# Two hand-overs between mixer and MLP, done by token block in a two-block decoder kernel

## What is computed

```python
# first block
y = mixer(rmsnorm(x, norm_mix_pre), ...)              # ends in  y @ w_out
x = x + rmsnorm(y, norm_mix_post)                     # hand-over 1
h = rmsnorm(x, norm_ffn_pre)
u = dwconv3(h @ w_up, conv_w)                         # 1024 -> 2 x 2816, width-3 taps over tokens
gate, val = jnp.split(u, 2, axis=-1)
y = (jax.nn.silu(gate) * val) @ w_down
x = x + rmsnorm(y, norm_ffn_post)                     # hand-over 2
# second block
proj = rmsnorm(x, norm_mix_g) @ w_in                  # its mixer goes on from here
```

## Time and profile before

| | us |
|---|---|
| median of 3 runs | 684.61 (683.48 to 685.54) |
| the profiled execution | 682.7 |
| its span, first to last instruction | 680.7 |
| TensorE busy | 637.0 (94%) |
| VectorE busy | 379.1 (56%) |
| ScalarE busy | 277.7 (41%) |
| GpSimd busy | 56.1 (8%) |

### The profile page before, as it was taken

The page is one execution under the profiler, slowest core; times in us unless marked ns, Lnnn a source line. Parts: engine busy times, 40 slices in busy tenths (PEclk is TensorE's granted clock), DMA queues, the critical chain, the costliest instruction groups (busy, mean ns, idle before and its releaser), DMA issues.

```text
span 680.7 us, 11095 instructions
## 1 busy us (share of the span) xinstructions
PE 637.0 (94%) x4347; PEld 482.7 (71%) x4347; DVE 379.1 (56%) x666; ACT 277.7 (41%) x431; POOL 56.1 (8%) x81
## 2 busy tenths in 40 slices
PE   7999999999999999999999999999999987668895
PEld 4999997799999999996598788744444432315364
DVE  5696965768766666666769456352222221203195
ACT  6763373656555555545774831220111110000193
POOL 1000000400000000002074620000000000000010
PEclk9999999999999999999999999999999998898998
DMA  9943542747655555302933448899899999999931
GB/s 323 328 172 126 194 141 67 267 149 243 235 186 185 185 185 186 128 0 101 392 142 123 139 172 320 350 430 428 354 430 430 425 425 428 428 428 427 405 128 62
DMA packets 55208, 174.75 MB, mean 257 GB/s; under 512 B 4742, under 2 KB 29442, under 8 KB 48898
## 3 DMA queue, kind: packets, MB, share of 16 engines
q1 hardware_dynamic: 54496, 172.54, 66.2%
q10 hardware_dynamic: 674, 1.69, 0.7%
HBM read 173.17 MB, written 1.05 MB: 256 GB/s over the span
## 4 chain that ended last, share of the span: by engine, by line
PE 73%; DMA 14%; DVE 7%; ACT 2%; issue 2%; another core or an unknown queue 0%; POOL 0%; POOLq 0%; DVEq 0%; ACTq 0%
PE ps L1809 15%; PE ps L1811 15%; PE ps L1810 15%; DMA W<-in_w_moe_dram 7%; DMA spare<-in_w_moe_dram 6%; PE ps L2326 6%; PE ps L2310 3%; PE ps L2386 3%; PE ps L2332 2%; PE ps L2006 2%; PE ps L1781 1%; PE ps L2433 1%; PE ps L2154 1%; DVE arena L1466 1%; PE ps L2105 1%
## 5 line engine op out<-in xcount | busy, mean ns | idle before, releaser
L1809 PE MATMUL ps<-hT_high,w_up_parts 128*128 128x256 f32 x352 | 99.9, 284 | 0.0
L1811 PE MATMUL ps<-hT_high,w_up_parts 128*128 128x256 f32 x352 | 99.7, 283 | 0.0
L1810 PE MATMUL ps<-hT_low,w_up_parts 128*128 128x256 f32 x352 | 99.7, 283 | 0.0
L1809 PEld LDWEIGHTS ps<-hT_high,w_up_parts 128*128 128x128 f32 x352 | 67.6, 192 | 0.5
L1810 PEld LDWEIGHTS ps<-hT_low,w_up_parts 128*128 128x128 f32 x352 | 67.6, 192 | 0.4
L1811 PEld LDWEIGHTS ps<-hT_high,w_up_parts 128*128 128x128 f32 x352 | 67.6, 192 | 0.0
L1297 DVE TENSOR_TENSOR w_up_parts<-W,w_up_parts 128x1024 fp32r<-128x1024 f32 x44 | 53.2, 1235 | 24.3 <-ACT w_up_parts L826 24.3
L826 ACT CAST w_up_parts<-W 128x1024 fp32r<-128x1024 f32 x44 | 44.7, 1047 | 28.5 <-PE ps L1811 28.5
L2326 PE MATMUL ps<-W,junk 128*32 128x512 f32 x368 | 46.2, 630 | 7.5 <-DMA W<-in_w_moe_dram 7.5
L996 ACT ACTIVATE sg<-ps 128x256 f32<-128x256 f32 x9 | 3.5, 384 | 121.4 <-PE ps L2326 121.4
L1809 PE MATMUL ps<-h_high,dense_high 128*128 128x256 f32 x160 | 45.8, 286 | 0.0
(11 more groups left out here) (480 smaller groups left out, 1318.7 us busy)
## 6 DMA issues: line engine op xcount, KB each, us to landing
W<-in_w_moe_dram SPq DMA_DIRECT2D x22, 2048.0 KB, 21.1
arena<-in_w_moe_dram SPq DMA_DIRECT2D x14, 2048.0 KB, 30.0
W<-in_w_up_dram SPq DMA_DIRECT2D x22, 1024.0 KB, 8.8
W<-in_w_in_dram SPq DMA_DIRECT2D x8, 2048.0 KB, 10.9
W<-in_w_down_dram SPq DMA_DIRECT2D x11, 1024.0 KB, 5.1
spare<-in_w_moe_dram SPq DMA_DIRECT2D x5, 2048.0 KB, 20.7
hh<-in_w_moe_dram SPq DMA_DIRECT2D x4, 2048.0 KB, 32.7
W<-in_w_out_dram SPq DMA_DIRECT2D x2, 2048.0 KB, 9.3
```

Source lines behind the costliest of these rows:

```text
L1809: pe.matmul(o, lhs[0], rhs[0], start=first, stop=False, skip_group_check=True)
L1810: pe.matmul(o, lhs[0], rhs[1], start=False, stop=False, skip_group_check=True)
L1811: return pe.matmul(o, lhs[1], rhs[0], start=False, stop=last_k, skip_group_check=True)
```

## The change

On TensorE the w_out products are ordered so that block 0 is complete after 60 of its 96 matmuls; block 0 is turned inside block 1's products, and the dummies go. The first MLP pair is not made by `up` any more: `up_tokens` has the tokens of one block stationary and 512 (block 0) or 2 x 256 (block 1) weight columns moving, ScalarE copies the result u out of PSUM into `junk` (`copy_up`), and `turn_up` turns it into the banks in which pair 0's taps read it. For block 0 that stands ahead of `turn_h(1, 1)`; block 1's last turns stand behind the first chunk of pair 1. The last two pairs' down products go by block, with those of the pair before (`down_before`) mixed in. In the second hand-over block 1 is turned within block 0's product, and that product begins with one written-out half. Dummies there: 4 ahead of the turn and 6 behind it. Both roots of a hand-over take the second half's sum as their bias. On VectorE the turned halves of block 0 are written out and lowered at the end of block 0's part (r = 0). Not shown in the diff: the new semaphores `u_done`, `uc_ready`, `u_turned`; y1's high part moves to another place in the arena; GpSimd builds its selection constants behind the split of pair 9 instead of behind `mlp_done` (its three edge fills stay there); pair 0's split is no longer cut in two, and `conv_mlp(0)` on ScalarE doesn't split pair 1, which is done ahead of it.

```diff
...
@@ -723,17 +723,17 @@
     act.wait_ge(sig("yms_ready"), n + 1)
-    act.activation(stat[:, 42 + 4 * r + b:43 + 4 * r + b], stat[:, 40 + 4 * r + b:41 + 4 * r + b], ACT.Sqrt)\
-       .then_inc(sig("ystd_ready"), 1)
-    if b == 1 and r == 0:
-        round_h(0)
+    act.wait_ge(sig("ysq_ready"), 2 * n + 2)
+    act.activation(stat[:, 42 + 4 * r + b:43 + 4 * r + b], stat[:, 40 + 4 * r + b:41 + 4 * r + b], ACT.Sqrt,
+                   bias=stat[:, 61:62]).then_inc(sig("ystd_ready"), 1)
...
     act.wait_ge(sig("xms_ready"), n + 1)
-    act.activation(stat[:, c + 2:c + 3], stat[:, c:c + 1], ACT.Sqrt).then_inc(sig("std_ready"), 1)
+    act.wait_ge(sig("xhsq_ready"), 2 * n + 2)
+    act.activation(stat[:, c + 2:c + 3], stat[:, c:c + 1], ACT.Sqrt, bias=stat[:, 63:64]).then_inc(sig("std_ready"), 1)
@@ -825,12 +825,28 @@
-split_up(0, 0, 0, (0, 1))
+split_up(0, 0, 0)
...
     hand_over(0, b)
-act.dma_start(gbc[:], a["norm_ffn_post"][0:1, :].broadcast_to([P, D])).then_inc(sig("gbc_landed"), 16)
-for j in range(1, 4):
-    round_h(j)
+    if b == 1:
+        act.dma_start(gbc[:], a["norm_ffn_post"][0:1, :].broadcast_to([P, D])).then_inc(sig("gbc_landed"), 16)
+    else:
+        round_h(0)
+        round_h(1)
+def copy_up(n, b, c0, c1):
+    act.wait_ge(sig("u_done"), at("u_done", n))
+    act.copy(junk[:, 512 * b + c0 * P:512 * b + c1 * P], ps[:, 5 if b and not c0 else 4, c0 * P:c1 * P]).then_inc(sig("uc_ready"), 1)
+copy_up(1, 0, 0, 4)
+round_h(2)
+round_h(3)
+copy_up(2, 1, 0, 2)
+split_up(1, 1, 0, (0, 1))
+copy_up(3, 1, 2, 4)
+split_up(1, 1, 0, (2, 3))
+act.wait_ge(sig("u_turned"), at("u_turned", 1))
@@ -868,13 +882,19 @@
 act.wait_ge(sig("down_landed0"), (NPAIR // 2) * 16 + 16)
-for i in range(2):
+def last_down(i):
...
     act.copy(last_dn[0][i], DN[0][:, i]).then_inc(sig("down_high"), 1)
+last_down(0)
+for i in range(2):
...
         act.activation(c[:, i, :], ps[:, i, 256 * g:256 * g + 256], ACT.Copy, scale=w).then_inc(sig("centre_done"), 1)
+    if i == 0:
+        last_down(1)
@@ -1129,12 +1149,11 @@
                 dve.wait_ge(sig("ysq_ready"), 2 * n + 1)
+                dve.tensor_scalar(stat[:, 40 + 4 * r + b:41 + 4 * r + b], stat[:, 60:61], EPS, None,
+                                  ALU.add).then_inc(sig("yms_ready"), 1)
...
                               ALU.mult).then_inc(sig("yg_ready"), 1)
-        dve.wait_ge(sig("ysq_ready"), 2 * n + 2)
-        dve.scalar_tensor_tensor(stat[:, 40 + 4 * r + b:41 + 4 * r + b], stat[:, 60:61], EPS, stat[:, 61:62], ALU.add,
-                                 ALU.add).then_inc(sig("yms_ready"), 1)
-        if b == 1:
+        if b == 1 and r == 1:
@@ -1147,18 +1166,21 @@
         c = 4 * (r + 1) + b
-        dve.wait_ge(sig("xhsq_ready"), 2 * n + 2)
-        dve.scalar_tensor_tensor(stat[:, c:c + 1], stat[:, 62:63], EPS, stat[:, 63:64], ALU.add,
-                                 ALU.add).then_inc(sig("xms_ready"), 1)
-        if b == 1 and r == 0:
-            lower_h(0)
+        dve.wait_ge(sig("xhsq_ready"), 2 * n + 1)
+        dve.tensor_scalar(stat[:, c:c + 1], stat[:, 62:63], EPS, None, ALU.add).then_inc(sig("xms_ready"), 1)
...
                           ALU.mult).then_inc(sig("hn_ready"), 1)
-    turn_out(r + 1, gain, 2)
-    turn_out(r + 1, gain, 3)
+        if r == 0:
+            for j in (2 * b, 2 * b + 1):
+                turn_out(r + 1, gain, j)
+            for j in (2 * b, 2 * b + 1):
+                lower_h(j)
+    if r == 1:
+        turn_out(r + 1, gain, 2)
+        turn_out(r + 1, gain, 3)
@@ -1928,42 +1953,75 @@
 pe.wait_ge(sig("sgo_ready"), at("sgo_ready", 2))
-for half in range(2):
-    for b in range(TB):
-        for k in range(4):
-            pe.wait_ge(sig("dense_low"), 4 * (6 + half) + k // 2 + 1)
-            product(ps[:, 4 + 2 * b + half, :], [t[:, k, b * P:(b + 1) * P] for t in y1],
-                    [t[:, k, :] for t in panel_hl(6 + half)], k == 0, False)
-for b in range(TB):
-    pe.wait_ge(sig("y1_low"), b + 2)
-    for half in range(2):
-        for k in range(4, KD):
-            pe.wait_ge(sig("dense_low"), 4 * (6 + half) + k // 2 + 1)
-            last = product(ps[:, 4 + 2 * b + half, :], [t[:, k, b * P:(b + 1) * P] for t in y1],
-                           [t[:, k, :] for t in panel_hl(6 + half)], False, k == KD - 1)
-    last.then_inc(sig("y_done"), 1)
+def out_rows(b, half, ks):
+    for k in ks:
+        pe.wait_ge(sig("dense_low"), 4 * (6 + half) + k // 2 + 1)
+        last = product(ps[:, 4 + 2 * b + half, :], [t[:, k, b * P:(b + 1) * P] for t in y1],
+                       [t[:, k, :] for t in panel_hl(6 + half)], k == 0, k == KD - 1)
+    return last
+out_rows(0, 0, range(4))
+out_rows(1, 0, range(4))
+out_rows(0, 1, range(4))
+pe.wait_ge(sig("y1_low"), 2)
+out_rows(0, 0, range(4, KD))
+out_rows(0, 1, range(4, KD)).then_inc(sig("y_done"), 1)
+out_rows(1, 1, range(4))
+pe.wait_ge(sig("y1_low"), 3)
+out_rows(1, 0, range(4, KD))
 turn_h(1, 0)
-keep_busy(3, 8)
-for k in range(24):
-    pe.matmul(ps[:, 3, 0:P], y1[0][:, k % KD, 0:P], y1[0][:, k % KD, 0:P], start=True, stop=True, skip_group_check=True)
+out_rows(1, 1, range(4, KD)).then_inc(sig("y_done"), 1)
+u_tok = v3(junk[:], TB)
+def up_tokens(b, c0, c1):
+    pe.wait_ge(sig("up_low"), c1)
+    for k in range(KD):
+        if k % 4 == 0:
+            pe.wait_ge(sig("hT_low"), 2 * b + k // 4 + 1)
+        last = product(ps[:, 5 if b and not c0 else 4, c0 * P:c1 * P], [t[:, k, b * P:(b + 1) * P] for t in hT_hl],
+                       [t[:, c0:c1, k, :] for t in w_up_hl], k == 0, k == KD - 1)
+    return last
+def turn_up(b, c0, c1):
+    for c in range(c0, c1):
+        i, g = divmod(c, 2)
+        last = pe.transpose(ps[:, i, 256 * g + b * P:256 * g + (b + 1) * P], u_tok[:, b, c * P:(c + 1) * P], ident[:])
+    return last
+up_tokens(0, 0, 4).then_inc(sig("u_done"), 1)
 turn_h(1, 1)
-pe.wait_ge(sig("hT_ready"), 4 + 2)
-keep_busy(0, 8)
 pe.wait_ge(sig("x_ready"), 2)
-for n in range(4):
-    pe.matmul(ps[:, 4 + n, :], zb[:, 0:P], zb[:], start=True, stop=False, skip_group_check=True)
-def up(p, q):
-    if not (isinstance(p, int) and p == 0):
-        pe.wait_ge(sig("tap_done"), p * 8 - 7)
+for n in range(2):
+    pe.matmul(ps[:, 6 + n, :], zb[:, 0:P], zb[:], start=True, stop=False, skip_group_check=True)
+pe.wait_ge(sig("uc_ready"), at("uc_ready", 1))
+turn_up(0, 0, 4)
+for h in range(2):
+    last = up_tokens(1, 2 * h, 2 * h + 2)
+    last.then_inc(sig("u_done"), 1)
+    pe.sem_inc(sig("up_used"), 2)
+def last_turns():
+    pe.wait_ge(sig("uc_ready"), at("uc_ready", 2))
+    turn_up(1, 0, 2)
+    pe.wait_ge(sig("uc_ready"), at("uc_ready", 3))
+    turn_up(1, 2, 4).then_inc(sig("u_turned"), 1)
+    for n in range(2):
+        pe.matmul(ps[:, 4 + n, :], zb[:, 0:P], zb[:], start=True, stop=False, skip_group_check=True)
+def up(p, q, behind_first=None):
+    pe.wait_ge(sig("tap_done"), p * 8 - 7)
     for c in range(4):
+        if c == 1 and behind_first:
+            behind_first()
...
         for k in range(KD):
-            if isinstance(p, int) and p == 0 and c == 0 and k % 4 == 0:
-                pe.wait_ge(sig("hT_low"), 3 + k // 4)
@@ -1978,31 +2036,59 @@
 pe.sem_inc(sig("down_used"), 1)
-up(0, 0)
-with pe.Fori(0, NPAIR // 2) as i:
+up(1, 1, last_turns)
+down(0, 0)
+up(2, 0)
+down(1, 1)
+with pe.Fori(1, NPAIR // 2 - 1) as i:
...
     down(i * 2 + 1, 1)
-for b in range(TB):
-    for i in range(2):
-        pe.wait_ge(sig("uact_low"), NPAIR + i)
-        pe.wait_ge(sig("down_low"), 2 * (NPAIR - 1) + i + 1)
-        for half in range(2):
-            last = product(ps[:, 4 + 2 * b + half, :], [t[:, 0, i, b * P:(b + 1) * P] for t in uact_hl],
-                           [t[i][:, 512 * half:512 * half + 512] for t in last_dn], False, True)
-    last.then_inc(sig("y_done"), 1)
+up(NPAIR - 2, 1)
+down(NPAIR - 3, 0)
+up(NPAIR - 1, 0)
+def down_before(b, i, halves):
+    pe.wait_ge(sig("uact_low"), NPAIR - 1)
+    pe.wait_ge(sig("down_low"), 2 * (NPAIR - 2) + i + 1)
+    for half in halves:
+        product(ps[:, 4 + 2 * b + half, :], [t[:, 1, i, b * P:(b + 1) * P] for t in uact_hl],
+                [t[:, i, 512 * half:512 * half + 512] for t in w_dn_hl], False, True)
+def down_last(b, i):
+    pe.wait_ge(sig("uact_low"), NPAIR + i)
+    pe.wait_ge(sig("down_low"), 2 * (NPAIR - 1) + i + 1)
+    for half in range(2):
+        last = product(ps[:, 4 + 2 * b + half, :], [t[:, 0, i, b * P:(b + 1) * P] for t in uact_hl],
+                       [t[i][:, 512 * half:512 * half + 512] for t in last_dn], False, True)
+    return last
+down_before(0, 0, range(2))
+down_before(0, 1, range(2))
+down_last(0, 0)
+down_before(1, 0, range(2))
+down_before(1, 1, range(1))
+down_last(0, 1).then_inc(sig("y_done"), 1)
+down_before(1, 1, range(1, 2))
+down_last(1, 0)
+down_last(1, 1).then_inc(sig("y_done"), 1)
...
 pe.wait_ge(sig("a2_landed"), 16)
-keep_busy(0, 16)
-for b in range(TB):
-    turn_h(2, b)
-    pe.wait_ge(sig("hT_ready"), 4 * 2 + 2 * b + 2)
+keep_busy(0, 4)
+turn_h(2, 0)
+keep_busy(3, 6)
```

(5 more changed lines are left out.)

28 lines of the change are left out of this document (12 added, 16 removed).

## The result

| | before | changed |
|---|---|---|
| median of the runs | 684.74 us (683.48 to 685.54) | 674.01 us (673.63 to 674.45) |
| ratio to before, 95% interval | | 0.9841 [0.9826, 0.9856] |
| profiled execution (span) | 682.7 (680.7) | 674.45 (672.4) |

Faster by 10.7 us in the medians and by 8.3 us between the two profiled executions. The forecast was 677.0, its range 674.0 to 681.5: 3 us too high, and the time lies at the range's lower edge (as a share of before it is just past it: 0.9841 against 674.0 / 684.61 = 0.9845). The gain of 10.7 us is also more than the 9.5 that the prediction gave as its upper bound.

What follows compares the result with a forecast made beforehand. Experts were taken as bound by weights, the MLP by TensorE, with two hand-overs leaving TensorE without useful work. Gains 5.1 + 2.5 = 7.6 us off 682.7 give 675.1, plus 1.9 to the median: 677.0, range 674.0 to 681.5.

Steps and rivals of the forecast that it cites:

- the last step of the sum: From the expected profiled execution, 675.1 us, to the median: 1.9 us added as in the kernel before, giving 677.0.
- the upper bounds of both hand-overs: Most that the two hand-overs could gain: 6 us in the first and 3.5 in the second, up to 9.5.
- First hand-over: From w_out to the MLP: first down product at 147.8 instead of 152.98, gain 5.1 us, bounds 3 to 6.
- The wait in (g): First MLP pairs: first down product waits 1.3 us for pair 0's lowered activation, whose taps now follow pair 1's split.
- The roots: Chain inside both hand-overs: VectorE's sum ahead of each root goes, 0.2 us each, twice per block; 5.6 us becomes 5.2.
- Second hand-over: From the MLP to mixer 2: xm products begin at 334.35 instead of 336.86, gain 2.5 us, bounds 0.5 to 3.5.
- GpSimd's constants: Moved into the MLP, about 274.5: 2.2 us of delay against 5.2 us of slack, so free; x updates undisturbed.
- SyncE's late reload: Reload for pair 2 issued at 137.2 instead of 135.96, landing at 146: hidden, with 5 us or so to spare.
- One gain only: Rival: second hand-over's gain is lost in the mixer behind it, or half of the first is; 679.5 us, chance 0.22.
- nothing arrives: Rival: the weight stream takes back the lead, or fuller first hand-over queues lag 5 us; 684.6 us, chance 0.08.
- Slower, by the clock: Rival: with forty dummies gone, TensorE's clock falls in pairs 0 and 1, costing up to 17 us; 694 us, chance 0.05.

Runs made afterwards that it cites:

- after_again: The changed kernel, unchanged, timed and profiled once more: 674.36 us, ratio 0.9851.
- old_order: Changed kernel with 12 w_out products moved ahead, so y's block 0 is complete after 72 products, not 60: 678.74 us, ratio 0.9913.
- no_C: Changed kernel with GpSimd's selection constants built after the end of the MLP again, as before: 675.58 us, ratio 0.9867.
- early_taps: Changed kernel with VectorE's copy of pair 0's conv taps ahead of pair 1's split and block 1's turns inside chunk 0: 673.28 us, ratio 0.9845.
- no_A: Kernel before with all of the change but the first hand-over's part: 680.29 us, ratio 0.9933.
- no_B: Changed kernel with the end of the MLP and the entry of mixer 2 ordered as before: 677.68 us, ratio 0.9886.
- no_fill: Changed kernel without the 4 and 6 dummies of the second hand-over: 675.82 us, ratio 0.9885.
- before_again: The kernel before, unchanged, timed and profiled again: 684.72 us, ratio 1.0001; its profiled execution took 683.34.
- cut2_before: Kernel before ended after mixer 2, with routing, experts and the last stage left out: 443.17 us.
- cut2_after: Changed kernel ended after mixer 2, with routing, experts and the last stage left out: 433.64 us.

## Why the prediction was off, point by point

- **What failed: the last step of the sum.** "The median of the runs is 684.61, 1.9 above that execution, so I forecast 677.0" carried a distance between profiled execution and median over to a kernel where it doesn't exist: the changed kernel's median is 0.4 below its profiled execution (0.2 above it in after_again). The sum against the profiled execution gave 675.1; measured were 674.45 for the profiled execution and 674.01 for the median. So 0.7 of the miss of 3.0 lies in the terms and 2.3 in this step. The bounds carried the same 1.9: the upper bounds of both hand-overs, 9.5, give 673.2 from the profiled execution. Why the kernel before is slower in its timed executions than in its profiled ones stays open in the main; the stretch in mixer 2 is the one candidate found, for 1.0 to 1.1 us.
- **First hand-over: right, 5.1 worked out, 5.37 measured.** The mechanism came as described: y complete at 110.66 and 119.98 (110.85, 120.2), stationary-token products without a wait, taps at 139.84 (139.9), first down product at 147.69 (147.8). The wait in (g) was 0.91, not 1.3. old_order shows what it rests on: the order of 12 products, and a TensorE that doesn't wait long enough there to lose its clock.
- **The roots: wrong in size.** 5.2 us were forecast for the chain of a block, from ScalarE's first square to the end of hn. It is 115.55 + 0.72 - 110.66 = 5.61, and before it was 118.62 + 0.72 - 113.65 = 5.69: 0.08 saved, not 0.4. The step held that the root starts earlier and costs the same; it starts 0.14 earlier and costs 0.09 more. That block 0's turn still began at 116.09, where 116.1 had been worked out for hn, is luck in part: y was complete 0.19 earlier, and the turn began when VectorE's half of hn was done (L1174: 115.55 + 0.49 = 116.04) and didn't wait for ScalarE's (116.27).

```profile
113.65 0.60 ACT L723 ACTIVATE junk<-ps 128x512 f32<-128x512 f32 x1 [8.85 <-PE ps L1811]
```

- **Second hand-over: right, 2.5 worked out, 2.80 measured.** 1.56 of it up to the first wA product (1.6 worked out), 1.24 in the entry (0.9): two tails of a product group were counted where only one stands. Here too two errors met: the chain of block 0 was 0.4 us longer than worked out, and the first product followed hn after 2.0 us (315.97 - 313.93), not 2.3.
- **GpSimd's constants: free, as said.** They ran at 269.29 and no down product waited. All eight updates of x took 745 to 753 ns; back behind the MLP they cost 0.64 in the trace (no_C).

```profile
L1165 DVE SCALAR_TENSOR_TENSOR x_tok<-hh,stat,x_tok x8: 745/748/753, 112.8 to 317.3; 128x512 f32<-128x512 f32 x8
```

- **SyncE's late reload: hidden, but with less to spare.** The ScalarE row of early_taps above shows it as the next thing that binds: with the first down product 1.08 us earlier, the next pair was already 0.28 late, so what was left to spare was about 0.8 us (an estimate, 1.08 - 0.28), not the "5 us or so" of the prediction.
- **Rivals.** "One gain only" and "nothing arrives" didn't come: no_A and no_B show both gains, and the experts didn't take them back. "Slower, by the clock" didn't come, but its mechanism is real: no_fill lost 2.6 us to it, old_order part of its 4.3. Its price was set too high: the falls seen last 3.2 to 6.8 us and cost 1.0 to 2.6, and no row bears the 17 us of the rival. It was right to look at the gaps and wrong to look only at the changed kernel: before has clocks that fall in some executions too (1.6 us in before_again). The Trainium skill (TensorE: Matmul & The Clock Gate, HAM oscillation) says that a stream broken by waits falls back; the trace agrees after gaps of 2.75, 2.16 and 1.13 us, and not after the 1.12 of the earlier trace rows; after the same 1.63 us at the start it agrees in three executions of 19, and in mixer 2 the clock falls where the 28 us ahead have no gap longer than 0.31 us.

## What to carry to other kernels

Where work by block follows a long chain, first ask in which order the producing engine should finish: moving twelve products decided over more than every shortened link of the chain, since it also kept TensorE from a wait in which its clock fell. Make the sum against the profiled execution and forecast the median from it only after asking what the other executions have that the profiled one hasn't; a spread of the runs (2 us before, 0.8 after), or a profiled execution below all of them, is a warning that they carry a cost which the page can't show, and the change may keep it or not. When a difference is in no trace, cutting both programs at the same places narrows it down faster than one theory after another, but a place is found only if the cut kernels' timed executions can be told apart by it.

## What was unexpected of the hardware

- The granted clock falls to 0.50 at the same products in one kernel and not in another, with the same work ahead of them for 30 us (366.8 to 370.0 us in cut2_before, none in cut2_after), and after one of two gaps of 1.12 and 1.13 us. It cost 1.0 to 1.6 us in these cases. At the start of the kernel it falls in three of 19 executions behind one and the same gap of 1.63 us, and 16 products take 5.34 us instead of 3.65.
- A ScalarE root of 128x1 takes 0.29 us with a bias read from memory and 0.20 without.
- The same kernel had medians of 684.7 and 682.9 us in different sessions, with runs up to 2.6 us from the one and up to 0.7 us from the other.
